# Reversed chunks: two chunks' keys in one stationary operand, in the recurrent heads of a float32 encoder layer

## What is computed

```python
def _hgrn2_chunk_step(state, inp):
    q, k, g, v = inp
    G = jnp.cumsum(g, axis=2)
    diff = G[:, :, :, None, :] - G[:, :, None, :, :]
    decay = jnp.where(causal, jnp.exp(jnp.minimum(diff, 0.0)), 0.0)
    A = jnp.einsum('bhid,bhijd,bhjd->bhij', q, decay, k)
    o = jnp.einsum('bhij,bhje->bhie', A, v) + jnp.einsum('bhid,bhde->bhie', q * jnp.exp(G), state)
    state = jnp.exp(G_last[:, :, 0, :])[..., None] * state + \
        jnp.einsum('bhjd,bhje->bhde', k * jnp.exp(G_last - G), v)
    return state, o
# forget = lb + (1 - lb) * sigmoid(f); g = log(forget); k = (1 - lb) * sigmoid(-f); v is i; q is silu(q)
```

## Time and profile before

| what | value |
|---|---|
| median of 3 runs | 2878.49 us (2878.25 to 2878.85) |
| the profiled execution's own time | 2877.56 us |
| its span in the trace | 2875.8 us |
| granted TensorE clock, mean | 0.998 of 2.4 GHz |
| busy: TensorE, weight loads, VectorE, ScalarE, GpSimd | 2854.4, 2379.4, 1523.7, 723.9, 196.9 us |
| level matmuls (line 1088) | 768 records |

### The profile page before, as it was taken

How to read it: one execution, slowest core, us unless ns; L and a number is a source line. 1 busy time by engine, 2 the same in 40 slices (tenths; PEclk the granted TensorE clock), 3 DMA queues, 4 the chain that set the end, 5 groups by cost and what they waited for, 6 DMA issues and landing times.

```text
span 2875.8 us, 33314 instructions
## 1 busy us (share of the span) xinstructions
PE 2854.4 (99%) x13264; PEld 2379.4 (83%) x13264; DVE 1523.7 (53%) x2879; ACT 723.9 (25%) x986; POOL 196.9 (7%) x87
## 2 busy tenths in 40 slices
PE   8999999999999999999999999999999999999998
PEld 7888888888888888888888888888888888888886
DVE  6886677756366345553346634555334663455521
ACT  5332344433122113221112111222111220222200
POOL 4333400025000000000000000000000000000000
PEclk9999999999999999999999999999999999999999
DMA  8667988889634465556563455555656345555554
GB/s 320 222 219 245 313 287 287 294 320 321 241 136 152 175 215 190 192 197 233 212 219 132 147 187 211 195 197 191 234 206 218 135 144 199 209 192 190 192 211 168
DMA packets 121977, 614.58 MB, mean 214 GB/s; under 512 B 13536, under 2 KB 13792, under 8 KB 74080
## 3 DMA queue, kind: packets, MB, share of 16 engines
q1 hardware_dynamic: 121824, 612.46, 60.8%
HBM read 474.00 MB, written 138.41 MB: 213 GB/s over the span
## 4 chain that ended last, share of the span: by engine, by line
PE 97%; DMA 1%; DVE 1%; POOL 0%; ACT 0%; issue 0%; POOLq 0%; SPq 0%; DVEq 0%; ACTq 0%
PE bank L1021 28%; PE bank L1022 28%; PE bank L1026 28%; PE bank L1088 3%; PE bank L1075 2%; PE bank L1077 2%; PE bank L1076 2%; PE bank L1159 1%; DMA raw<-w_units 1%; PE bank L1190 1%; PE bank L1182 1%; PE bank L1176 1%; PE bank L1180 0%; PE bank L1187 0%; PE bank L1035 0%; PE bank L1032 0%
## 5 line engine op out<-in xcount | busy, mean ns | idle before, releaser
L1021 PE MATMUL bank<-h_hi,w_both 128*128 128x512 f32 x2400 | 944.6, 394 | 0.0
L1022 PE MATMUL bank<-h_lo,w_both 128*128 128x512 f32 x2400 | 934.2, 389 | 0.0
L1026 PE MATMUL bank<-h_hi,w_both 128*128 128x512 f32 x2400 | 593.4, 389 | 0.0
L1021 PEld LDWEIGHTS bank<-h_hi,w_both 128*128 128x128 f32 x2400 | 450.5, 188 | 97.2 <-issue 3.8
L1022 PEld LDWEIGHTS bank<-h_lo,w_both 128*128 128x128 f32 x2400 | 450.6, 188 | 96.2 <-issue 3.8
L1026 PEld LDWEIGHTS bank<-h_hi,w_both 128*128 128x128 f32 x2400 | 450.5, 188 | 93.5
L939 DVE TENSOR_TENSOR z<-bank,rms_inv 128x512 f32<-128x512 f32 x176 | 121.8, 692 | 338.8 <-PE bank L1026 338.3
L1022 PE MATMUL bank<-g_lo,w_both 128*128 128x512 f32 x704 | 273.9, 389 | 0.0
L1021 PE MATMUL bank<-g_hi,w_both 128*128 128x512 f32 x704 | 273.9, 389 | 0.0
L952 DVE SCALAR_TENSOR_TENSOR conv<-z,params,conv 128x512 f32<-128x512 f32 x352 | 263.5, 750 | 6.2
L413 POOL TENSOR_TENSOR w_both<-raw,w_both 128x1024 fp32r<-128x1024 f32 x80 | 195.7, 2446 | 522.3 <-ACT w_both L427 471.1
(11 more groups left out here) (220 smaller groups left out, 3136.5 us busy)
## 6 DMA issues: line engine op xcount, KB each, us to landing
w_both<-w_split SPq DMA_DIRECT2D x372, 1024.0 KB, 4.8
w_split<-w_both SPq DMA_DIRECT2D x248, 512.0 KB, 5.7
raw<-w_units SPq DMA_DIRECT2D x124, 512.0 KB, 5.4
x_in<-x_t SPq DMA_DIRECT2D x32, 256.0 KB, 5.5
res<-x_t SPq DMA_DIRECT2D x32, 256.0 KB, 5.1
out<-res SPq DMA_DIRECT2D x32, 256.0 KB, 6.5
masks<-masks_in SPq DMA_DIRECT2D x1, 1152.0 KB, 8.3
gm_w<-gm_wt SPq DMA_DIRECT2D x1, 256.0 KB, 6.3
```

The costliest lines, as they stand in the source:

```text
L1021: pe.matmul(dst, w_hi[slot][:, off + k, :], rhs_hi(k), start=first and k == 0, stop=False)
L1022: pe.matmul(dst, w_hi[slot][:, off + k, :], rhs_lo(k), start=False, stop=False)
L1026: mm = pe.matmul(dst, w_lo[slot][:, off + k, :], rhs_hi(k), start=False, stop=last and k == n - 1)
```

## The change

Chunks 1 and 3 of a tile run backwards in time. Then the first halves of the runs of 2s in chunk 0, in time, and the mirrored ones in chunk 1 lie on complementary places, and `k_first[s]` holds both in 128 columns. One matmul makes a level for a pair of chunks: the stationary operand is the pair's 128 keys, the moving one both chunks' queries, 2x64 columns. The chunks lie in the order 0, 2, 1, 3 (`lain`).

```diff
+def half_of(ap, s, second):
+    part, (step, width) = ap.ap
+    return bass.AP(ap.tensor, ap.offset + (s if second else 0),
+                   (part, (width // 2 + (-s if second else s), 2), (2 * s, width // (4 * s)), (1, s)))
...
-                dve.tensor_tensor(q0, blocks(sig_q[:, :], P), blocks(bank[1][:, :], P), ALU.mult).then_inc(evac[1], 1)
+                for n, (sig, q) in enumerate(zip(by_parity(sig_q[:, :]), by_parity(bank[1][:, :]))):
+                    op = dve.tensor_tensor(q0[:, n * (NC // 2):(n + 1) * (NC // 2), :], sig, q, ALU.mult)
+                op.then_inc(evac[1], 1)
...
-                    dve.tensor_tensor(k2_l, k_l, spread(t_r, s), ALU.mult).then_inc(*head_dve.did(f"kl{2 * s}"))
-                    dve.tensor_copy(k2_r, k_r).then_inc(*head_dve.did(f"kr{2 * s}"))
+                    if s == 1:
+                        dve.tensor_copy(half_of(k_all[:, :], s, True),
+                                        half_of(kp[:, :], s, True)).then_inc(*head_dve.did("kr2"))
+                        k_l = half_of(kp[:, :], s, False)
+                    else:
+                        k_l = interleaved(k_first[s][:, :], s)
+                        dve.tensor_copy(k_l, half_of(k_all[:, :], s, False)).then_inc(*head_dve.did(f"kc{s}"))
+                        then(f"kc{s}")
+                    dve.tensor_tensor(half_of(k_all[:, :], s, False), k_l, spread(t_r, s),
+                                      ALU.mult).then_inc(*head_dve.did(f"kl{2 * s}"))
...
         def level(s):
-            dst, rows = level_out(s), P // 2 if s == P // 2 else P
-            for c in range(NC):
-                mm = pe.matmul(dst[0:rows, c * P // 2:(c + 1) * P // 2], kp[s][:, c * P:c * P + rows],
-                               q_right[s][:, c * P // 2:(c + 1) * P // 2], start=True, stop=True)
+            for pair in range(NC // 2):
+                dst, q_r = (ap.rearrange("p (a n) -> p a n", a=2)[:, :, pair * P // 2:(pair + 1) * P // 2]
+                            for ap in (level_out(s), q_right[s][:, :]))
+                mm = pe.matmul(dst, k_first[s][:, pair * P:(pair + 1) * P], q_r, start=True, stop=True)
...
+        def backwards(hi, lo):
+            for dst, src in ((back_hi, hi), (back_lo, lo)):
+                v = src[:, :, :].bitcast(F32).rearrange("p k (n a q) -> p k n a q", a=2, q=P)
+                dve.tensor_copy(dst[:, :, :, :], v[:, :, :, 1, ::-1]).then_inc(back_made, 1)
...
+                    if u == 6:
+                        for n, s in enumerate(LEVELS):
+                            sp.dma_start(level_masks[s:P, n, 1, :], level_masks_in[0:P - s, n, 1, :]).then_inc(masks_here, 16)
+                            sp.dma_start(level_masks[0:s, n, 1, :], level_masks_in[s:2 * s, n, 1, :]).then_inc(masks_here, 16)
```

More of the change, by code:

```diff
@@ L34 @@
 DOWN_SPLIT = [0, 8, 15, KF]
-I_BANKS = (2, 3, 0, 1)
+V_BANKS = (2, 3, 0, 1)
 B_TOK = 1
@@ L74, in before, with by_parity, parities, lain @@
         return self.sem, turn * len(self.names) + self.head_start
-def halves(ap, s):
-    v = ap.rearrange("p (n two s) -> p n two s", two=2, s=s)
-    return v[:, :, 0, :], v[:, :, 1, :]
+def by_parity(ap):
+    v = ap.rearrange("p (n a q) -> p n a q", a=2, q=P)
+    return v[:, :, 0, :], v[:, :, 1, ::-1]
+def parities(ap):
+    v = ap.rearrange("p (a n q) -> p a n q", a=2, q=P)
+    return v[:, 0, :, :], v[:, 1, :, :]
+def lain(c):
+    return c % 2 * (NC // 2) + c // 2
+def half_of(ap, s, second):
+    part, (step, width) = ap.ap
+    assert step == 1
+    return bass.AP(ap.tensor, ap.offset + (s if second else 0),
+                   (part, (width // 2 + (-s if second else s), 2), (2 * s, width // (4 * s)), (1, s)))
+def interleaved(ap, s):
+    part, (step, width) = ap.ap
+    assert step == 1
+    return bass.AP(ap.tensor, ap.offset, (part, (s, 2), (2 * s, width // (2 * s)), (1, s)))
 def blocks(ap, s):
@@ L161, in build @@
     qp = place("qp", [P, TT], F32, y_at)
-    kp = {s: place(f"kp{s}", [P, TT], F32, y_at + (1 + n) * BLK)
-          for n, s in enumerate(LEVELS + [P])}
+    kp, k_all = place("kp", [P, TT], F32, y_at + BLK), place("k_all", [P, TT], F32, y_at + 2 * BLK)
+    k_first = {s: place(f"k_first{s}", [P, TT // 2], F32, y_at + 3 * BLK + n * BLK // 2)
+               for n, s in enumerate(LEVELS) if s > 1}
     q_both = place("q_both", [P, NC, P + P // 2], F32, y_at + 9 * BLK)
@@ L177, in build @@
     hx_lo = place("hx_lo", [P, KD, TT], F32R, y_at + KD * BLK)
+    back_hi = place("back_hi", [P, KD, NC // 2, P], F32R, arena)
+    back_lo = place("back_lo", [P, KD, NC // 2, P], F32R, arena + KD // 2 * BLK)
     u_act = place("u_act", [P, NH, TT], F32, y_at + 16 * BLK)
@@ L286, in build @@
         at += TT // 2
+    level_masks, level_masks_in = (m.rearrange("p (n a q) -> p n a q", a=2, q=P)
+                                   for m in (masks[:, TT:], masks_in[:, TT:]))
+    N_MASKS = 16 * (2 + 2 * len(LEVELS))
     level_place = {64: (5, 0), 32: (5, 1), 16: (6, 0), 8: (6, 1), 4: (7, 0), 2: (7, 1)}
@@ L713, in _ @@
             pre_sum(0, c + 1)
+        dve.wait_ge(*pre_dve.before(KD))
+        dve.tensor_copy(blocks(sum_r[:, 0:TT // 2], P), by_parity(sum_n[:, :])[1]).then_inc(sums_back, 1)
+        backwards(hx_hi, hx_lo)
         dve.wait_ge(ident_here, 16)
@@ L769, in _ @@
                 dve.wait_ge(evac[0], used + 1)
-                dve.tensor_scalar(kp[1][:, :], sig_nf[:, :], keep, None, ALU.mult).then_inc(*head_dve.did("k"))
+                for dst, src in zip(parities(kp[:, :]), by_parity(sig_nf[:, :])):
+                    op = dve.tensor_scalar(dst, src, keep, None, ALU.mult)
+                op.then_inc(*head_dve.did("k"))
                 dve.wait_ge(*head_act.at("sig_f", it))
-                dve.tensor_scalar(total[1][:, :], sig_f[:, :], keep, lower[:, 2, bass.ds(h, 1)], ALU.mult,
-                                  ALU.add).then_inc(*head_dve.did("forget"))
+                for dst, src in zip(parities(total[1][:, :]), by_parity(sig_f[:, :])):
+                    op = dve.tensor_scalar(dst, src, keep, lower[:, 2, bass.ds(h, 1)], ALU.mult, ALU.add)
+                op.then_inc(*head_dve.did("forget"))
                 then("forget")
@@ L1100, in for_first_tokens @@
                     cols = slice((k % 2) * NC, (k % 2 + 1) * NC)
-                    if is_i and not lower:
+                    if is_v and not lower:
                         pe.wait_ge(hx_hi_made, k + 1)
```

145 lines of the change are left out of this document (85 added, 60 removed).

## The result

The changed kernel takes 2855.42 us (median of 4 runs, 2853.82 to 2860.36), the kernel before beside it 2878.67 us. The ratio is 0.992, 95% interval 0.9905 to 0.9939: faster by 23.3 us, where 23.9 were forecast. The profiled execution took 2856.65 us with a span of 2854.9.

What follows compares the result with a forecast made beforehand. TensorE's queue and its waits were taken to bound the kernel. From 2877.56 us, -28.2 + 3.4 + 0.5 + 0.5 = -23.8 gave 2853.7, and 0.93 us for the median gave 2854.6 us; range 2851 to 2866, chance 0.62.

Steps and rivals of the forecast that it cites:

- The level block: Each head's level matmuls: 24 records in place of 48, 2.67 us for 5.02; 28.2 us less over tiles 1 to 3.
- Twice the columns cost 6% more: Tile 1 records on TensorE: 0.111 us with 128 columns against 0.105 with 64, so fewer, wider matmuls pay.
- A: VectorE time added per head from sig_q to m64: 0.85 us, bounds 0.5 and 2.45.
- Tile 0's heads: Four heads of tile 0: TensorE's gain becomes waiting and VectorE's path grows by A, +3.4 us (+2.0 to +9.8).
- no further collision is added: Tile 0, VectorE against GpSimd: the last GpSimd operation in the path is the one of 86.25; no cost added.
- rival (c): TensorE's clock falls to 1.2 GHz at tile 0's waits, some 2 us per head, +8: 2862.6 us; chance 0.07.
- The start: Start of tile 0: two more column sums cost +0.5 us; the backward copies are covered and cost 0.
- The masks: SP's queue at units 5 and 6: more DMAs, 6 us late, reach TensorE as 0.5 us; bounds 0 and 3.
- (a): New patterns on VectorE are dearer, A = 2.45; tile 0 costs 9.8 us, not 3.4: 2861.0 us; chance 0.14.
- (d): VectorE's path also bounds tiles 1 to 3; slower than before from A = 5.7; 2883.1 us at A = 6; chance 0.04.
- (e): Level block: two-run matmul streams no faster, 0.163 us per record, 13.2 us less, 4.4 more: 2869.6 us; chance 0.05.
- (b): Start of tile 0: the 127-row mask DMA delays unit 9, then unit 10, +3 to +5 us: 2858.6; chance 0.08.

Runs made afterwards that it cites:

- e1: Changed kernel with the pairing alone undone, four matmuls of 64 columns in each level from 2: 2886.81 us.
- e3: Changed kernel with each head's four v_head operations done twice on VectorE: 2864.00 us.
- e7: Changed kernel with each head's four v_head operations done seven times on VectorE: 2903.95 us.
- e12: Changed kernel with single mask DMA, v_head a head ahead, four of six lower halves per tile 0 head on VectorE, and pairing undone: 2882.40 us.
- e11: Kernel before with four of each head's six lower halves in tile 0 made by VectorE instead of GpSimd: 2878.26 us.

## Why the prediction was right, step by step

- **Bound and place of the gain:** right. TensorE's own queue sets the time, VectorE's path has slack in tiles 1 to 3 and, once the levels are paired, none in tile 0 (e1, e3, e7, e12). One reading under it was wrong: "in tile 0 the chain on VectorE already ends last, by 0.1 us". In e11 m64 ends 1.3 us earlier (138.77 us against 140.11 in the second head) and tile 0's heads stay at 44.36 us, so TensorE was the last there too and the 0.1 us between the tiles' heads has another cause. The two paths were level within that, which is why TensorE's gain in tile 0 still became waiting.
- **The level block:** right (2.67 forecast, 2.68). The term was still 0.19 us a head too small: it compared the blocks alone and not the record behind them, 0.43 us before and 0.23 now. 12 x 0.19 = 2.3 us. Of it 0.6 us isn't seen in the span; from tile 1's first level block to the end the changed kernel took 2046.2 us and seven other kernels with paired levels 2044.8 to 2046.1, so that much differs between executions. "Twice the columns cost 6% more" was misread: the 0.105 us was a mean over records of 0.111 and some of 0.07 us with a stationary operand of 64 columns, and e1 shows 0.111 at 64 columns.
- **A:** right in size, 0.74 us in tile 1. In tile 0 sig_q to m64 went from 26.93 to 27.80 us in the second head, +0.87. The negative step costs the copies nothing that shows: 1.22 us for `back_hi`, where the forecast had 1.2 us at the copies' usual rate and 2.3 at half of it. VectorE's idle time ahead of the state update was forecast at 2.5 us and is 4.2: I took the 2.35 us off 4.95 and forgot that VectorE, too, waits less for the levels. The 3.3 us beside it were right.
- **Tile 0's heads:** the mechanism of the waits right (period 45.0 to 45.4 forecast, 45.20 in head 1), the term mis-sized, 3.4 against 5.7 us. The step that failed is "no further collision is added": it looked at the operations between sig_q and m64, and the collision came to the copy right behind m64, which A pushed past GpSimd's next start. Head 2 pays 1.5 us more for it. Head 0 pays 0.4 more, with rival (c)'s clock.
- **The start:** column sums right (0.5 forecast, 0.4). The masks were mis-sized, 0.5 against 1.1 us in the profiled execution and up to 4.5 in other kernels with the same DMAs; their upper bound of 3 was too low as well, because SP was priced by the only row at hand, 0.43 us a DMA, and one DMA took eight times that. The clock at 28 us (1.6 us) had been left out; rival (c) looked for it in the heads only.
- **The rivals:** (a), (d) and (e) did not come. (b) and (c) both came in part; that the too small gain nearly cancels them is luck. They probably also spread the changed kernel's runs over 6.5 us: its two longer runs (2856.65 and 2860.36) have a mean clock of 0.996 and the two shorter ones (2853.82 and 2854.19) one of 0.998. For the masks only the starts of other kernels' executions speak.

## What to carry to other kernels

Count matmuls and not columns when stationary operands are full and the moving ones short (measured here in float32, with 64 and 128 columns). When TensorE gets faster, look at what the operation *behind* the last one on a helper engine's path will now run into, not only at the path. And ask of each helper which engine stands still for it: work moved from GpSimd to the busier VectorE made VectorE's path shorter, and the kernel faster only where VectorE was the bound.

## What the runs showed of the hardware

- While GpSimd runs its tensor operation (2.4 us), VectorE's operations with all operands in SBUF stand still to its end (2.32 us instead of 0.29; 1.65 instead of 0.69), and those that read PSUM don't (q0 at 163.00, 0.75 us for both halves, inside GpSimd's 162.56 to 164.96). The Trainium skill ("SBUF — State Buffer", "SBUF: two separate sides") calls it an exclusive lock on a shared port pair; the traces agree, in copies, in products and in a one-source operation (line 951 at 157.19, 2.62 instead of 0.43).
- Issuing one DMA of a single row, the second of fourteen, held SP for 3.5 to 5.5 us in all six kernels that have it, where the other thirteen took 0.25 to 0.59. Why isn't settled.
- TensorE's granted clock fell from 2.4 to 1.2 GHz (stretches of 0.5 to 0.9 in the mean) after waits of 0.5 to 1.8 us (and longer ones in e7) in some executions and not in others, with the same code ahead of it. It cost 0.4 to 1.6 us where one fall could be told apart. At the start the falls go with the longer waits in the kernels with the change; in the heads what decides is open.
